# Two mixers' modulation tiles: from the SyncE queue and one VectorE operation each to the GpSimd queue and two GpSimd operations each

## The reference, cut to what matters

```
cond = silu(c)
for l in range(2):
    mod = cond @ ada_w[l] + ada_b[l]            # [1024] @ [1024, 9 * 1024]
    sh1, sc1, g1, sh2, sc2, g2, sh3, sc3, g3 = split(mod, 9)
    h = h + 0.5 * g1 * swiglu(norm(h) * (1 + sc1) + sh1, ...)
    z = (norm(h) * (1 + sc2) + sh2) @ w_in[l]   # then four mixers: differential attention,
    h = h + g2 * (mixed @ w_out[l])             # convolution, gated MLP, forgetting attention
    h = h + 0.5 * g3 * swiglu(norm(h) * (1 + sc3) + sh3, ...)
```

## Time and profile before

| | before |
|---|---|
| times of three runs, us | 2295.28, 2298.12, 2299.72 (median 2298.12) |
| the profiled execution: its own time, us | 2294.87 |
| its span, us | 2293.1 |
| mean granted TensorE clock | 0.985 |
| PE busy, share of the span | 2223.0 us, 97% |
| DVE busy | 1586.1 us, 69% |
| ACT busy | 1097.4 us, 48% |
| POOL busy | 61.4 us, 3% |

### The profile page before, as it was taken

How to read it: one execution, slowest core, us unless ns; L and a number is a source line. 1 busy time by engine, 2 the same in 40 slices (tenths; PEclk the granted TensorE clock), 3 DMA queues, 4 the chain that set the end, 5 groups by cost and what they waited for, 6 DMA issues and landing times.

```text
span 2293.1 us, 31930 instructions
## 1 busy us (share of the span) xinstructions
PE 2223.0 (97%) x11865; PEld 1869.8 (82%) x11865; DVE 1586.1 (69%) x1885; ACT 1097.4 (48%) x1288; POOL 61.4 (3%) x90
## 2 busy tenths in 40 slices
PE   7999989999999999999999999999999999999998
PEld 6887877887788786788788799978878888998887
DVE  6886876885776786666655778675566557867555
ACT  4434654444434465434544464654444446565443
POOL 1000110000000110000000000000000000000000
PEclk8999998999999999999999999999999999999999
DMA  8986544886687473566465564356556555435653
GB/s 308 347 306 194 192 145 167 318 315 201 219 286 257 149 225 134 190 221 212 161 206 186 165 178 133 129 188 197 183 175 197 185 186 157 130 112 175 209 184 109
DMA packets 325042, 454.56 MB, mean 198 GB/s; under 512 B 32722, under 2 KB 270040, under 8 KB 324952
## 3 DMA queue, kind: packets, MB, share of 16 engines
q1 hardware_dynamic: 320952, 440.98, 57.9%
q0 software_dynamic: 3728, 11.31, 1.7%
q10 hardware_dynamic: 272, 1.05, 0.1%
HBM read 449.91 MB, written 1.05 MB: 197 GB/s over the span
## 4 chain that ended last, share of the span: by engine, by line
PE 86%; DVE 6%; ACT 4%; issue 2%; DMA 1%; SPq 1%; DVEq 0%; ACTq 0%
PE ps L612 20%; PE ps L614 20%; PE ps L613 20%; PE ps L605 5%; PE ps L606 4%; PE ps L607 4%; PE ps L775 2%; DVE wlo L1941 1%; PE ps L757 1%; ACT whi L1315 1%; PE ps L758 1%; PE ps L760 1%; PE ps L924 1%; PE ps L702 1%; PE ps L1032 1%
## 5 line engine op out<-in xcount | busy, mean ns | idle before, releaser
L1941 DVE TENSOR_TENSOR wlo<-raw,whi 128x2048 fp32r<-128x2048 f32 (+1 forms) x348 | 791.8, 2278 | 355.9 <-ACT whi L1315 354.6
L1315 ACT ACTIVATE whi<-raw 128x2048 fp32r<-128x2048 f32 x346 | 660.3, 1911 | 302.4 <-PE ps L614 242.5
L612 PE MATMUL ps<-whi,xl 128*128 128x512 f32 x1472 | 592.6, 403 | 0.0
L614 PE MATMUL ps<-whi,xh 128*128 128x512 f32 x1472 | 575.0, 391 | 0.0
L613 PE MATMUL ps<-wlo,xh 128*128 128x512 f32 x1472 | 574.8, 391 | 0.0
L612 PEld LDWEIGHTS ps<-whi,xl 128*128 128x128 f32 x1472 | 277.4, 188 | 61.8 <-issue 4.7
L614 PEld LDWEIGHTS ps<-whi,xh 128*128 128x128 f32 x1472 | 277.0, 188 | 60.0
L613 PEld LDWEIGHTS ps<-wlo,xh 128*128 128x128 f32 x1472 | 277.4, 188 | 58.6 <-issue 4.3
L605 PE MATMUL ps<-xl,whi 128*128 128x256 f32 x864 | 251.6, 291 | 1.6 <-DVE wlo L1941 1.6
L612 PE MATMUL ps<-whi,hidl 128*128 128x512 f32 x640 | 252.1, 394 | 0.4 <-DVE hidl L2133 0.4
L614 PE MATMUL ps<-whi,hidh 128*128 128x512 f32 x640 | 249.2, 389 | 0.0
(11 more groups left out here) (399 smaller groups left out, 2381.6 us busy)
## 6 DMA issues: line engine op xcount, KB each, us to landing
raw<-in_ffn_w_in_dram SPq DMA_DIRECT2D x176, 512.0 KB
arena<-in_ada_w_dram SPq DMA_DIRECT2D x144, 512.0 KB, 6.3
raw<-in_w_in_dram SPq DMA_DIRECT2D x54, 1024.0 KB
raw<-in_ffn_w_out_dram SPq DMA_DIRECT2D x44, 1024.0 KB
raw<-in_w_ffn_gate_dram SPq DMA_DIRECT2D x88, 512.0 KB
raw<-in_w_ffn_up_dram SPq DMA_DIRECT2D x88, 512.0 KB
raw<-in_w_ffn_down_dram SPq DMA_DIRECT2D x44, 1024.0 KB
raw<-in_w_out_dram SPq DMA_DIRECT2D x16, 1024.0 KB
```

The lines of the kernel that those rows point to most:

```text
L612: pe.matmul(o, al, wh, start=start, stop=False, **kw)
L614: return pe.matmul(o, ah, wh, start=False, stop=stop, **kw)
L1315: act.activation(whi[:, k % 3, :], raw[:, k % 3, :], ACT.Copy).then_inc(hi_done, 1)
L1941: tt(a[0], a[1], a[2].bitcast(F32), ALU.subtract).then_inc(lo_done, 1)
```

## The change

For the mixers n = 1 and n = 4 alone, the 16 tiles are loaded by POOL's queue and added by POOL. Each tile takes a `tensor_scalar` of 128 x 1024 in its own buffer (tile * cond), then a `tensor_tensor` that adds it to `acc`. The semaphores `tile_loaded` are new. A table `SP_TILES` takes into account how many tiles SP still loads ahead of each feed-forward. `tap_operands` stays first, tiles 0 to 7 come behind it, then `spread_rows`, then tiles 8 to 15.

```diff
+SP_TILES = {1: 0, 3: 24, 4: 48}
...
+        tile_loaded = [sem(f"tile_loaded{i}") for i in range(2)]
...
-                    def tiles(i):
-
-                        first = {3: 0, 4: 2, 6: 4, 8: 6, 9: 8, 10: 10, 11: 12, 12: 14}
-                        for q in range(first[i], first[i] + 2) if i in first else ():
-                            sp.wait_ge(adam_used, ADAM[m] + q + 1)
-                            sp.sem_inc(sp_waited, 1)
-                            at = 3072 * (m % 3) + 1024 * (q % 2)
-                            sp.dma_start(adam[:, q % 2, :], ada_chunks[(m // 3) * KC + q // 2, :, at:at + 1024]
-                                         ).then_inc(adam_loaded[q % 2], 16)
...
             def ada(m, q, two=0):
 
-                parts = 2 if m in (2, 5) else 3
-                at, k = q % 2, 2 * two + q // parts
-                dve.wait_ge(adam_loaded[at], (16 * (ADAM[m] // 2 + q // 2 + 1)) + 48 * two)
+                at, k = q % 2, 2 * two + q // 3
+                dve.wait_ge(adam_loaded[at], (16 * (SP_TILES[m] // 2 + q // 2 + 1)) + 48 * two)
...
-                def tiles(first, last):
-                    for q in range(first, last):
-                        ada(m, q)
...
+            def modulation_tiles(n, first, last):
+
+                m = n + 1
+                for q in range(first, last):
+                    until(adam_used, ADAM[m] + q + 1)
+                    at = 3072 * (m % 3) + 1024 * (q % 2)
+                    pool.dma_start(adam[:, q % 2, :], ada_w[m // 3, P * (q // 2):P * (q // 2) + P, at:at + 1024]
+                                   ).then_inc(tile_loaded[q % 2], 16)
+                    if q > first:
+                        add_tile(m, q - 1)
+                add_tile(m, last - 1)
+
+            def add_tile(m, q):
+
+                pool.wait_ge(tile_loaded[q % 2], 16 * ((m // 3) * KC + q // 2 + 1))
+                if q == 0:
+                    pool.wait_ge(acc_init, 16 * m)
+                pool.wait_ge(adam_used, ADAM[m] + q + 2)
+                seg = acc[:, 1024 * (q % 2):1024 * (q % 2) + 1024]
+                st(pool.tensor_scalar(adam[:, q % 2, :], adam[:, q % 2, :], condT[:, 0, q // 2:q // 2 + 1], 0.0, ALU.mult,
+                                      ALU.add))
+                pool.tensor_tensor(seg, adam[:, q % 2, :], seg, ALU.add).then_inc(adam_used, 1)
...
                     tap_operands(n, n // 3)
+                    modulation_tiles(n, 0, 8)
                     spread_rows(n // 3)
+                    modulation_tiles(n, 8, 2 * KC)
```

More of the change, by code:

```diff
@@ L528, in _ @@
                                 load(L, k, whole(as8, k, cols8(w_in, l, col)))
-                            tiles(i)
                         for g in range(4):
                             load(L, k0 + 11 + g, whole(as2, k0 + 11 + g, rows2(w_out, l, ORDER[g], 4)))
-                            tiles(11 + g)
                     else:
@@ L2100, in ada @@
                 dve.wait_ge(adam_used, ADAM[m] + 6 * two + (q + 2))
-                seg = acc[:, 1024 * (q % parts):1024 * (q % parts) + 1024]
+                seg = acc[:, 1024 * (q % 3):1024 * (q % 3) + 1024]
                 scalar = condT[:, 0, bass.ds(k, 1)]
@@ L2480, in mix0 @@
                 lo(L, k0 + 2)
-                tiles(0, 2)
                 lo(L, k0 + 3)
-                tiles(2, 4)
                 lo(L, k0 + 4)
@@ L2516, in mix0 @@
                 lo(L, k0 + 6)
-                tiles(4, 6)
                 lo(L, k0 + 7)
@@ L2535, in mix0 @@
                 lo(L, k0 + 8)
-                tiles(6, 8)
                 copied(L, zi["cg"])
@@ L2545, in mix0 @@
                 logits(L, st, 0, S0, amask, 32 ** -0.5)
-                tiles(8, 10)
                 lo(L, k0 + 10)
@@ L2552, in mix0 @@
                 logits(L, st, 1, S1, amask, 32 ** -0.5)
-                tiles(10, 12)
                 lo(L, k0 + 11)
@@ L2565, in mix0 @@
                 gelu_in(2, zt["gu"], gu_tmp)
-                tiles(12, 13)
                 dve.wait_ge(s["gu_e"], 2 * l + 2)
@@ L2577, in mix0 @@
                     ALU.mult).then_inc(s["dout"], 1)
-                tiles(13, 14)
                 rest_out(L, 2, 0, 2, s0f[:, 1024:1536])
                 logits(L, st, 2, S1, amask, 1.0)
-                tiles(14, 16)
                 sums_of(L, st, 2)
```

## The result

The changed kernel took 2338.1 us (median of four runs, 2333.99 to 2343.42), against 2296.7 us of the kernel before beside it (four runs, 2295.1 to 2299.72): ratio 1.018, 95% interval 1.0162 to 1.0197. It is 41 us slower; the forecast was 8 us slower, with a range up to 2326.

What follows compares the result with a forecast made beforehand. PE bounds the kernel, busy 2223.0 of 2293.1 us. New waits of 10.6 us less 3.3 gained give +7.3, with clock nearer 8: 2302.9 from the profiled 2294.87, or 2306 for a median; range 2293 to 2326.

Steps and rivals of the forecast that it cites:

- What goes, VectorE: 32 additions leave DVE, 47.3 us, 23.7 a mixer; worth nothing by itself, since PE waits for none of them.
- What goes, SyncE: Weight loads no longer queue behind tile loads; shorter wait for ACT's squares and less slow clock gain 1.6 to 5, taken 3.3.
- What comes, GpSimd: Each mixer tile costs POOL 5.5 us, ends 4.2 and 7.2; no PE wait for the sum, but no slack.
- GpSimd comes last: Rival: at 6.5 us a tile PE waits 11 us for POOL in each mixer, 2331 us; chance 0.20.
- Cost to VectorE: POOL's SBUF reads block DVE up to 2.4 us a tile; at six tenths, 1.4 a tile, 23 a mixer.
- The new waits: PE waits at gated MLP's operand 2.3 us, convolution's mean 2, transposed probabilities 1: 5.3 a mixer, 10.6 in both.
- The clock: PE's clock loses something behind longer waits, moving the slowdown from +7.3 to nearer 8 us.
- Not slower: Rival: DVE's cover keeps the three new waits near 0, SyncE's gain of 3.3 to 5 stays, 2294 us; chance 0.14.
- both cancel: Rival: both parts are small or cancel, 2298 us, within 4.6; some 2 us of wait a mixer against 3.3 gained; chance 0.24.
- Slower: Sign of the whole kernel's time change: slower 0.60, against same 0.26 and faster 0.14.

Runs made afterwards that it cites:

- e1: Changed kernel without any modulation-tile work in both mixers, neither loads, scaling nor additions: 2295.8 us, ratio 0.9996 to the kernel before.
- e2: Changed kernel with the tile loads on GpSimd's queue kept, but no scaling and no addition: 2295.9 us, ratio 0.9994 to the kernel before.
- e12: Kernel before with only SyncE's list changed, its tile pairs from the fourth on issued one unit later: 2295.8 us, ratio 0.999 to the kernel before.
- e17: Changed kernel with GpSimd's addition cut into two pieces of 512 columns, eight tiles still ahead of the spreading: 2326.2 us, ratio 1.0121 to the kernel before.
- e15: Changed kernel with ten tiles instead of eight ahead of the convolution's spreading, nothing cut: 2335.1 us, ratio 1.0153 to the kernel before.
- e7: Changed kernel with zero matmuls filling two TensorE waits, 20 before the gated MLP's product, 16 before the first attention scores: 2330.9 us, ratio 1.0139.
- e5: Changed kernel without the addition, GpSimd doing the loads and the scaling alone: 2296.2 us, ratio 0.9993 to the kernel before.
- e3: Changed kernel with three memsets of the tile on GpSimd in place of scaling and addition: 2295.7 us, ratio 0.9992 to the kernel before.
- e9: Changed kernel with both GpSimd operations on a tile, scaling and addition, cut into four pieces of 256 columns: 2374.5 us, ratio 1.0339.

## Why the prediction was wrong, point by point

- **What goes, VectorE: worth nothing.** Right: e1, with no addition on DVE and none on POOL, is 1 us from the kernel before.
- **What goes, SyncE: 1.6 to 5 us, took 3.3.** The mechanism is right. ACT copies unit 10 without a wait for its load, PE's wait fell from 3.2 to 1.8 us, and the four matmuls behind it took 1.98 us instead of 3.63. The size is 1 to 2 us (e1, e2, e12), at the lower end of my bounds or under it.
- **What comes, GpSimd: 5.5 us a tile, no wait of PE.** Right. The first eight tiles ended at 301.9 us (forecast 299.5); from one to the next it took 4.4 to 7.8 us, 5.6 on average, and 5.0 for the last eight. PE had no wait for POOL. The parts: scaling 1.13 us undisturbed (taken 1.3), addition 2.34 to 2.40 (taken 2.7). The last sum ended at 375.9, later than the 358.4, since the spreading ahead of these tiles waited for PE's scores until 320.2 where I had 301.8; but PE was later still. The rival *GpSimd comes last* didn't come true here; e17, with the addition in halves, shows that it stood close, at some 6 us a tile.
- **Cost to VectorE: 1.4 us a tile, 23 us a mixer.** This is the first step that failed. Standing still was 60.4 us, 30 a mixer, 1.9 a tile, eight tenths of my 2.4 and not six. The addition's part, 56.8 / 32 = 1.8 us, is near the 1.6 that I read from the earlier trace rows; the scaling's, 11.8 / 32 = 0.4, is half of what I took. The factor of six tenths rested on no row but DVE's busy share, and it was wrong: I multiplied by the share of time for which DVE wants the port. But an instruction that is held waits for the rest of POOL's, however little it needs itself, so that a chain of short ones is caught again and again, for 1.4 and 2.1 us at L2489 and L2491 in the changed kernel.
- **The new waits, 5.3 us a mixer.** The second step that failed, and by more. PE's idle time grew by 22.7 us, 11 a mixer. At the gated MLP's operand I had 5.5 us of blocking and 2.3 of wait. In the first mixer the chain from the norm's subtraction on grew by 8.4 us, and it began 3.5 us later (262.01 to 265.46) where the mixer as a whole came 1.7 later (POOL's first product 248.46 against 246.74), so that the operand was late by 10.2 us. PE waited 4.6 us there, and 7.9 in the second mixer. At the convolution's mean I had 2, and it grew by 2.4 and 0.7; at the transposed probabilities I had 1, and 1.9 was measured in the first mixer. The largest one that I hadn't named is L914: the differential attention's operands wait behind the same list, 4.1 us in the first mixer and 1.8 in the second. I had looked for covers of a few us one by one, as if each began anew. Between L1202 and L914 DVE was held again (L1931, L2504, L2461), and PE waited at both.
- **The clock: from 7.3 to "nearer to 8".** The third, and the largest in proportion. PE was busy for 21.9 us more over the same matmuls in the profiled execution, and for 12.6 in e15. Not all of it need be lost time, since a PE that comes sooner can wait longer. What filling two of the waits gave back, 7 us, is the part that e7 shows; how much of the 41 us the clock costs in all stays open.
- **The rivals.** *Not slower* and *both cancel* are refuted for the change; they describe e5, in which 11.8 us of standing still, spread over the list, cost nothing: ahead of the gated MLP's operand 2.4 us, under the rival's 3.2.
- **Slower** was the likeliest sign and came; the time is outside my range, since all three terms of the loss erred in the same direction, and I had summed their ends as if the clock were a remainder.

Of the two pages of the Trainium skill cited there, the first (SBUF — State Buffer, Who interferes with whom) says that a DVE instruction with at most one SBUF input, outside the 2-port modes, is left alone, and this is now shown for one: L1941, whose other input is in PSUM, takes 1.20 us in the changed kernel, beside an addition of POOL, and took 1.20 in the one before. The second (Trainium skill, GPSIMD Engine Reference, Engine selection), which spoke against the change, was right in its advice. The estimate of 2.2 us from the figure of this page of the Trainium skill lies near the 2.34 measured. But POOL had the time for it, and the price stands on DVE.

## What to carry to other kernels

Ask of an operation moved to GpSimd not only how long it takes there, but how long one instruction of it holds VectorE, and how many VectorE instructions stand in the list ahead of the next thing that TensorE waits for: each of them, however small, can pay the whole length. One-input work and loads were free here by themselves, a two-input add was not, and beside it the one-input work wasn't free either. If the add must be there, cut it only as far as GpSimd keeps its own times. And where TensorE gets new waits, price the clock as a term of its own, not as a remainder: filling two waits gave back 7 of the 41 us.

## What the runs showed of the hardware that was not expected

- A memset on GpSimd, which reads nothing, left VectorE's two-input operations alone but not its `TENSOR_SCALAR`. With 109 us more of POOL's busy time in e3 than in e1 (168.0 against 59.0), most of it memsets, the wide subtraction stayed at 2287 ns, and of DVE's groups in the first mixer only one grew by over 0.1 us: the norm's last step, 410 ns in e1 (the first row) and 987 in e3 (the second). In the second mixer five groups grew by as much, all of them `TENSOR_SCALAR`. Two are of 128 x 2 elements, L2485 and L2486, which took 1.00 and 0.98 us instead of 0.15 and 0.17 and ended within 0.02 us of a memset's end.

```profile
L2495 DVE TENSOR_SCALAR arena<-arena,lnmv,lnr 128x256 f32<-128x256 f32 x2 | 0.7, 410 | 0.0
```

```profile
L2495 DVE TENSOR_SCALAR arena<-arena,lnmv,lnr 128x256 f32<-128x256 f32 x2 | 1.9, 987 | 0.0
```

- The two-input addition, alone on GpSimd, held VectorE for two thirds of its own mean length (1.8 of 2.73 us), the scaling for a quarter (0.37 of 1.45). Why the scaling's share is so much smaller stays open; no run tries it.
- A GpSimd instruction has a fixed part, so that cutting costs. In e9 a scaling of 256 columns that nothing held took 0.48 us and such an addition 0.74, where 1024 columns took 1.13 and 2.34: from the two widths, an estimate of 0.2 to 0.3 us of each doesn't depend on the columns.

```profile
256.98 0.48 POOL L2667 TENSOR_SCALAR arena<-arena,condT 128x256 f32<-128x256 f32 x1 [3.31 <-DMA arena<-in_ada_w_dram]
...
262.15 0.74 POOL L2668 TENSOR_TENSOR arena<-arena 128x256 f32<-128x256 f32 x1
```
